# Expert gathers of a decoder step issued from a loop on GpSimd, with rings of 8 and 8 rows

## What is computed

```python
def block_fn(hb):                       # 128 tokens
    q = (hb @ w_q).reshape(PEER_BLOCK, PEER_HEADS, 2, PEER_QDIM // 2).astype(jnp.float32)
    s = jnp.einsum('thpd,phkd->thpk', q, sub_keys.astype(jnp.float32))
    s1, i1 = lax.top_k(s[:, :, 0], PEER_TOPK)
    s2, i2 = lax.top_k(s[:, :, 1], PEER_TOPK)
    ...
    top_s, top_pos = lax.top_k(cand, PEER_TOPK)
    e = jnp.take_along_axis(cidx, top_pos, axis=-1)
    g = jax.nn.softmax(top_s, axis=-1)
    act = jax.nn.gelu(jnp.einsum('thkd,td->thk', u_tab[e], hb).astype(jnp.float32))
    return jnp.einsum('thk,thkd->td', (g * act).astype(hb.dtype), v_tab[e])
```

## Time and profile before

| | us |
|---|---|
| three timed runs: median (lowest to highest) | 1338.03 (1335.47 to 1338.72) |
| the profiled execution, its own time | 1336.01 |
| its span, first to last instruction | 1334.0 |
| first gather starts | 487.89 |
| last gather starts | 1313.11 |

### The profile page before, as it was taken

How to read it: one execution, slowest core, us unless ns; L and a number is a source line. 1 busy time by engine, 2 the same in 40 slices (tenths; PEclk the granted TensorE clock), 3 DMA queues, 4 the chain that set the end, 5 groups by cost and what they waited for, 6 DMA issues and landing times.

```text
span 1334.0 us, 12747 instructions
## 1 busy us (share of the span) xinstructions
PE 1061.0 (80%) x3429; PEld 548.1 (41%) x3429; DVE 711.6 (53%) x1713; ACT 236.3 (18%) x570; POOL 654.9 (49%) x787
## 2 busy tenths in 40 slices
PE   6798888997899895888876877777767777777777
PEld 3346666665577574344322322222222222222223
DVE  3157453887132264688566465457665564443432
ACT  1111221112300210321211211101112112111010
POOL 3333334332000026566666666666666666676663
PEclk9798898998999898888988889899999898999989
DMA  7643341795033569799999999999999999999995
GB/s 241 206 168 105 108 134 48 248 319 164 9 96 126 189 230 384 272 351 357 376 370 369 376 355 369 372 369 398 379 364 366 360 371 370 374 392 356 367 365 215
DMA packets 126412, 379.87 MB, mean 285 GB/s; under 512 B 14284, under 2 KB 23624, under 8 KB 126356
## 3 DMA queue, kind: packets, MB, share of 16 engines
q0 software_dynamic: 89408, 312.89, 61.8%
q1 hardware_dynamic: 36948, 66.29, 14.8%
HBM read 377.55 MB, written 1.59 MB: 284 GB/s over the span
## 4 chain that ended last, share of the span: by engine, by line
PE 46%; POOL 17%; issue 13%; DVE 9%; another core or an unknown queue 6%; DMA 6%; ACT 3%; SPq 0%; DVEq 0%; ACTq 0%; POOLq 0%
PE twoD L838 8%; PE twoD L840 8%; POOL big L966 8%; PE twoA L523 7%; POOL big L955 7%; PE twoA L789 4%; DMA big<-peer_v,oT 3%; PE twoD L740 2%; DVE big L1616 2%; POOL r L955 2%; PE twoA L500 2%; PE twoA L663 1%; PE twoA L460 1%; PE twoD L618 1%
## 5 line engine op out<-in xcount | busy, mean ns | idle before, releaser
L955 POOL DMA_INDIRECT big<-peer_u,oT x232 | 218.8, 943 | 251.3 <-DVEq L1572 165.1
L966 POOL DMA_INDIRECT big<-peer_v,oT x262 | 249.0, 950 | 153.4 <-remote 77.0
L1616 DVE CUSTOM_DVE_ANT_0 big<-big,twoA 128x1024 f32<-128x1024 f32 x128 | 155.2, 1218 | 135.2 <-DMA big<-peer_u,oT 94.1
L1616 DVE CUSTOM_DVE_ANT_0 big<-big,twoD 128x1024 f32<-128x1024 f32 x104 | 124.9, 1214 | 54.5 <-DMA big<-peer_u,oT 28.7
L838 PE MATMUL twoD<-big 128*128 128x512 f32 x176 | 102.1, 659 | 49.7 <-issue 23.1
L523 PE MATMUL twoA<-hT,big 128*128 128x288 f32 x448 | 115.0, 417 | 0.0
L838 PE MATMUL twoD<-big,modT 128*128 128x512 f32 x132 | 79.2, 676 | 39.1 <-DMA big<-peer_v,oT 19.6
L840 PE MATMUL twoD<-big 128*128 128x512 f32 x176 | 96.6, 627 | 8.6 <-issue 8.4
L523 PEld LDWEIGHTS twoA<-hT,big 128*128 128x128 f32 x448 | 86.5, 196 | 24.4 <-issue 0.8
L840 PE MATMUL twoD<-big,modT 128*128 128x512 f32 x132 | 75.9, 654 | 11.6 <-issue 11.4
L838 PEld LDWEIGHTS twoD<-big 128*128 128x128 f32 x176 | 30.7, 199 | 112.8 <-issue 57.9
(11 more groups left out here) (328 smaller groups left out, 1635.9 us busy)
## 6 DMA issues: line engine op xcount, KB each, us to landing
big<-w_ada SPq DMA_DIRECT2D x12, 2048.0 KB, 8.8
big<-w_in SPq DMA_DIRECT2D x5, 2048.0 KB, 8.0
big<-w_in SPq DMA_DIRECT2D x9, 1024.0 KB, 11.3
big<-peer_w_q SPq DMA_DIRECT2D x3, 2048.0 KB, 9.4
big<-peer_v,oT POOLq DMA_INDIRECT x262
big<-cache_v POOLq DMA_DIRECT2D x64, 64.0 KB, 2.1
big<-w_out SPq DMA_DIRECT2D x2, 2048.0 KB, 7.8
big<-peer_u,oT POOLq DMA_INDIRECT x232
```

The source lines that it names most:

```text
L955: pool.indirect_dma_start(urows[i % NU], None, peer_u, bass.IndirectOffsetOnAxis(ap=eidx[:, t, s:s + 1], axis=0)).then_inc(u_in[i % NU], 16)
L966: pool.indirect_dma_start(vrows[j % NV], None, peer_v, bass.IndirectOffsetOnAxis(ap=eidx[:, t, s:s + 1], axis=0)).then_inc(v_in[j % NV], 16)
L1616: dve.tensor_tensor_reduce(out=urows[i % NU], in0=urows[i % NU], in1=h2tok[t][:, :], scale=1.0, scalar=0.0, op0=ALU.mult, op1=ALU.add, acc ...
```

## The change

The rings become 8 and 8 rows, all in `big`. POOL no longer runs an unrolled list: it issues the first 16 u gathers, waits until every weight of the last projection has been used, and then runs an engine loop of 16 passes. A pass has 16 pairs of u(p + 16) and v(p), so v is 16 rounds behind u all through the loop. The last 16 u and the last 32 v follow unrolled, with v catching up. An instruction in a loop can't name another column of `eidx` in each pass, so each stream has a table of 16 columns in `oT`: DVE copies 8 columns at a time into `ucur` (`u_index`), and ACT into `vcur` (`v_index`).

The waits change with it. u(q) waits for `u_used` >= q - 7. v(j) waits for `v_used` >= j + 1, where ACT raises `v_used` by 8 once, behind `exps(0)`; counted in rounds that is j - 7, and no v gather goes ahead of `exps(0)`. `v_index(c+1)`, which stands ahead of `gelus(c+1)` on ACT, waits until round 8c - 1 has been multiplied, which is `v_used` >= 8c counted in rounds. `weigh(c)` now stands behind the dot 8(c+1) + 1.

```diff
-        NU, NV = 10, 11
+        NU, NV = 8, 8
-        LAG, NEAR = 18, 8
+        LAG = 16
...
+            def gather_v(p):
+
+                pool.indirect_dma_start(vrows[p % NV], None, peer_v, bass.IndirectOffsetOnAxis(
+                    ap=vcur[:, p % LAG:p % LAG + 1], axis=0)).then_inc(v_in[p % NV], 16)
...
+            for p in range(LAG):
+                if p % CHUNK == 0:
+                    pool.wait_ge(ucur_ready, p // CHUNK + 1)
+                if p >= NU:
+                    pool.wait_ge(u_used, p - NU + 1)
+                gather_u(p)
+            for g in last_in:
+                pool.wait_ge(*released[g])
+            with pool.Fori(0, ROUNDS // LAG - 2) as i:
+                for p in range(LAG):
...
+                    pool.wait_ge(u_used, i * LAG + (LAG + p - NU + 1))
+                    pool.sem_inc(row_asked, 1)
+                    gather_u(p)
...
+                    pool.wait_ge(v_used, i * LAG + (p + 1))
+                    pool.sem_inc(row_asked, 1)
+                    gather_v(p)
...
             exps(0)
+            act.sem_inc(v_used, NV)
...
+            def v_index(c):
+
+                t, first = slots[c * CHUNK]
+                act.wait_ge(routed, c * CHUNK // (2 * HEAD) + 1)
+                if c >= 2:
+                    act.wait_ge(v_used, NV + (c - 1) * CHUNK)
+                L.tell(act.activation(vcur[:, c % 2 * CHUNK:(c % 2 + 1) * CHUNK], eidx[:, t, first:first + CHUNK], ACT.Copy),
+                       vcur_ready, wait=False)
...
                 if j % CHUNK == CHUNK - 1 and j + 1 < ROUNDS:
+                    v_index(c + 1)
                     gelus(c + 1)
...
+                if i % CHUNK == CHUNK - 1 and i // CHUNK + 2 < ROUNDS // CHUNK:
+                    u_index(i // CHUNK + 2)
+                if i % CHUNK == 1 and i >= CHUNK:
                     weigh(i // CHUNK - 1)
```

More of the change, by code:

```diff
@@ L192, in layer_program @@
         diag = [big[:, NUB * D + 512 + i * P:NUB * D + 512 + (i + 1) * P] for i in range(4)]
-        vrows = [big[:, (NUB + 1 + i) * D:(NUB + 2 + i) * D] for i in range(NV - 1)]
-        v_wring = [0 if (NUB + 2 + i) * D <= o else (1 if (NUB + 2 + i) * D <= o + WSLOT else 2) for i in range(NV - 1)] + [3]
+        vrows = [big[:, (NUB + 1 + i) * D:(NUB + 2 + i) * D] for i in range(NV)]
         diag += [cT[:, 4 * i:4 * i + 4, :].rearrange("p c b -> p (c b)") for i in range(2)]
@@ L271, in layer_program @@
         x1tok = part(3 * D, 0).rearrange("p (t d) -> p t d", d=D)
[L272 to L275, removed]
+        g2tok = part(2 * D, 4 * D).rearrange("p (t d) -> p t d", d=D)
+        yout = part(D, 8 * D)
         adaG = yout.rearrange("p (g n) -> p g n", n=512)
@@ L970, in _, with gather_u @@
[L970 to L978, removed]
+            def gather_u(p):
+                pool.indirect_dma_start(urows[p % NU], None, peer_u, bass.IndirectOffsetOnAxis(
+                    ap=ucur[:, p % LAG:p % LAG + 1], axis=0)).then_inc(u_in[p % NU], 16)
@@ new lines, in _ @@
+            j = ROUNDS - 2 * LAG
+            for i in range(ROUNDS - LAG, ROUNDS):
+                if i % CHUNK == 0:
+                    pool.wait_ge(ucur_ready, i // CHUNK + 1)
+                pool.wait_ge(u_used, i - NU + 1)
+                gather_u(i)
+                while j <= (ROUNDS - CHUNK if i == ROUNDS - 1 else i - LAG + (i - ROUNDS + LAG) // 2):
+                    if j % CHUNK == 0:
+                        pool.wait_ge(vcur_ready, j // CHUNK + 1)
+                    pool.wait_ge(v_used, j + 1)
+                    gather_v(j)
+                    j += 1
@@ L981, in _ @@
+            for j in range(j, ROUNDS):
+                pool.wait_ge(v_used, j + 1)
+                gather_v(j)
         @block.scalar
@@ L1186, in gelus @@
                 L.tell(act.activation(chunk, chunk, ACT.Gelu_apprx_tanh), gelu_done, wait=False)
+            def v_index(c):
[5 more added lines that the diff above has]
+                       vcur_ready, wait=False)
+            v_index(0)
             gelus(0)
@@ L1195, in _ @@
                 if j >= NDG:
-                    act.wait_ge(v_used, j - NDG + 1)
+                    act.wait_ge(v_used, NV + j - NDG + 1)
                 act.activation(diag[j % NDG], ident, ACT.Copy, scale=dots[:, t, s:s + 1]).then_inc(diag_ready, 1)
@@ L1593, in output @@
             def output(t):
-                dve.wait_ge(v_used, sum(SLOTS[0:t + 1]))
+                dve.wait_ge(v_used, NV + sum(SLOTS[0:t + 1]))
                 if t:
@@ L1617, in dot, with u_index @@
                                          op0=ALU.mult, op1=ALU.add, accum_out=dots[:, t, s:s + 1]).then_inc(u_used, 1)
+            def u_index(c):
+                t, first = slots[c * CHUNK]
+                L.tell(cp(ucur[:, c % 2 * CHUNK:(c % 2 + 1) * CHUNK], eidx[:, t, first:first + CHUNK]), ucur_ready, wait=False)
             for _ in route(0):
                 pass
+            u_index(0)
+            u_index(1)
             found, router = 1, route(1)
```

29 lines of the change are left out of this document (10 added, 19 removed).

## The result

| median of 6 runs | us | lowest to highest |
|---|---|---|
| kernel before | 1338.38 | 1335.47 to 1340.48 |
| kernel after | 1351.53 | 1346.97 to 1353.52 |

The ratio is 1.0096, with a 95% interval from 1.0074 to 1.0119. The direction was forecast, the size was not: 64 us were expected and 13 came.

What follows compares the result with a forecast made beforehand. POOL's stalls for late v_used increments while the DMA engines are saturated were taken as the bound. Start +7.4 and stalls 136 + 17 - 95.9 = +57.1 on 1336.01 gave 1400.5, plus 2.0 for the median: 1402.5 us, range 1325 to 1460.

Steps and rivals of the forecast that it cites:

- What bounds the kernel: POOL outpaces the DMA engines; v gathers stall for v_used increments made late by the backlog: 95.9 us in 24 places.
- The rings: v gathers on POOL need v_used three rounds sooner: stalls one in about 8 rounds, 34 x 4.0 = 136 us.
- The restart: The loop's wait is its own instruction, the gather dispatched after it: 0.5 us a stall, 34 x 0.5 = 17 us.
- The tables: Index copies on DVE and ACT cost nothing; v_index's wait mostly falls into the same stall: 0, up to 15 us.
- The start: Fewer gathers go out before the weights are used, but peerq blocks and v(0) come sooner: +7.4 us, -3 to +19.
- The u ring: 8 u rows for 10 leave three rounds of slack and the v wait binds first: nothing, up to 10 us.
- the issue of a gather in a loop: POOL's register instructions cost nothing where its queue is filled: 0, bounds 0 to 0.36 us a gather.
- the tail: Ten v gathers behind the last u, against nine: 0 to 2 us.
- Stalls stay as rare as they were: Rival: POOL's stalls stay at 24 places, of 4.5 us each, plus the start: 1357 us; 15%.
- The transfers are the bound: Rival: 370 GB/s is all the DMA engines have, stalls only move queued work, time stays at 1338 us; 3%.

Runs made afterwards that it cites:

- pace_v_b: Kernel before with a MEMSET of 128x128 ahead of each v gather, on a chip where before takes 1337.73 us: +1.2 us.
- half_pe_c: Kernel before with the first of PE's two matmuls left out in 7 rounds of 8, where before takes 1337.73 us: -8.7 us.
- rings8_late: Kernel before, unrolled, no tables, with 8 u and 8 v rows and v gathers started as late as in after; before 1337.73 us: +1.7 us.
- late_v: Kernel before with only the v start moved: v(0) behind 17 u gathers, all weights used and exps(0); before 1341.86 us: +6.8 us.
- unrolled: Kernel after with the engine loop written out, waits on the gathers against constants; +8.3 us against before at 1257.46, repeated +9.1 against 1257.23.
- unrolled_v3: Kernel after with its loop written out and a v table of 24 columns for 16, v_index waiting for eight rounds less; before 1257.23 us: +9.2 us.
- rings8: Kernel before, unrolled with its old lags, with 8 u and 8 v rows for 10 and 11; before 1257.46 us: +0.3 us.

## Why the prediction was wrong in size

**What bounds the kernel** was right for this chip: stalls of 4 us in which v gathers wait for increments of `v_used` that PE's records show long before. It was half right as to the cause. Busy DMA engines alone don't do it (409 GB/s and 0.04 us on chip A), nor a backlog (17.5 us from issue to landing on chip A, and pace_v_b), nor, as far as chip A and half_pe_c tell, PE's work. It goes with the chip, or with what was different on it at the time. The 93.7 us of stalls, less some 20 that gathers 1.28 us apart and not 1.2425 take on the fast kind, are about the 80 us between the two.

**The rings, +57.1 with the restart: this step failed.** It replayed a cycle of before with the times of the increments held fixed and lowered the threshold by three rounds. The times aren't fixed. In before the increment that a stalled gather needs shows some 22 us late, in after some 15, three rounds less; it is as late as the ring lets it be, and comes when POOL has stopped and all but about one gather has been moved. The term was 34 places x 4.0, 136 us, one in 8 rounds; after measured 28 x 3.75, 105 us, one in 9.7. With rings8_late, which has the rings and neither tables nor loop, it is 24 places as in before, so the rings have none of it that these runs can tell. (The low end of the forecast's own range, 1365 at one in 10 rounds, is 1372 by its terms: 27.2 x 4.5 - 95.9 + 7.4.) The sign that was missed stands in the earlier trace rows: increments 105 to 107 came 4.9 and 9.1 us apart and then all at once. A series that ends in a burst tells when something was let go, not when each step was done, and can't be replayed against another threshold.

**The restart, +17 of these (34 x 0.5)** looks right where the trace shows it. Diagonal 116 and v(112) need the same 105: ACT starts at 851.50 and POOL at 852.29, 0.79 later; `v_index` and v(111) need 104, 845.21 and 845.94, 0.73 later. In before the same pair was 0.23 apart. The traces' semaphore events say the same: from the first increment of the burst to the v gather it is 0.26 us in 27 of before's 28 stalls ahead of v, in 24 of late_v's 26 and 27 of rings8_late's 30, and 0.82 us in 14 of after's 26 and 20 of the 29 on chip B. Some 0.56 us at each of 28 stalls is 16 us at most; the stalls grew by 11.4, and on chip B they are 12.6 us more than late_v's and the time 10. On a chip without stalls it is worth the measured 1.2. But unrolled wasn't run on a chip that stalls. The longer restart is measured; that it, and not the tables, is what the stalls grew by is the likeliest reading and not shown.

**The tables** were put at 0, up to 15. On chip E the place of `v_index`'s wait was worth 0.1 us (unrolled_v3); no run took the copies themselves out. On a chip that stalls `v_index` held ACT for 19.40 us and DVE for 8.56, ending 0.7 us before the start of a v gather that had waited for the same value. In after the stalls stand more often ahead of u (32.1 us for 5.5; 15.8 in rings8_late with the same rings) and less ahead of v. How much of the 11.4 the tables have stays open.

**The start, +7.4 between -3 and +19**: measured about +5.0, with 3.3 of it before the first gather, which the prediction has no term for and which other kernels show without the change. So the number came near in part by luck. v(0) was expected at 531 behind 17 u gathers and came at 527.89 behind 17. The `peerq` blocks come on time, as argued: PE's last record and ACT's last copy are 0.04 us apart, where before had 7.7:

```profile
511.08 11.81 PE L789 MATMUL twoA<-hT,r 128*128 128x288 f32 x48
...
522.93 0.41 ACT L1175 ACTIVATE r<-twoA 128x288 f32<-128x288 f32 x1 [3.47 <-PE twoA L789]
```

On the fast kind, where rings8 (old order at the start) is not late there, the same start costs 8 to 10 us.

**The u ring, the issue of a gather in a loop, the tail**: the first two were put at 0. Gathers stay 1.24 us apart, and rings8_late, with both rings smaller, has no more stalls than late_v, though 15.8 us of them for 9.3 stand ahead of u. The tail, 0 to 2, came out 1.3 shorter. No stall falls on each 16th pair, so no branch is seen.

**The rivals.** "Stalls stay as rare as they were", 1357 with 15%, is nearest to what happened, 5 us from the result. Its argument was the right one: the replay rests on increments that came under the old spacing. Its number is partly luck: 24 x 4.5 = 108 for 28 x 3.75 = 105. "The transfers are the bound", 3%, was put as 370 GB/s being all there is, and the stretch at 412 GB/s dismissed that rightly for this chip; on three of five chips the transfers are the bound, at 409.

**Open**: what delays the increments on some chips, and whether it is the chip at all or something beside this core; whether a pace that leaves the DMA engines idle in between (390 GB/s) would end the stalls there; what sets the 12 to 15 rounds between the long stalls; and how the 11.4 us divide between separate waits and tables.

## What to carry over

A stall whose end is a burst of late signals did not get more frequent here in step with a tighter threshold: before sizing such a term, look whether the signals came one by one as the work was done, or together when something was let go. Where one transfer resource fills a whole stage, first price what a change leaves unmoved at its start; that term was there on both kinds of chip. And run the kernel before on a second chip before explaining its stalls by its program.

## What the chip showed

- One unchanged kernel, 1257 to 1259 us on three chips and 1338 to 1342 on two and on that of the result, the executions on each within 0.6%. The DMA engines moved 409 GB/s over 500 us on the first kind and 370 on the other, where in saturated stretches they also reach 412.
- PE's increments reached ACT 0.04 us after PE's record on the first kind with the DMA engines at 409 GB/s, and 23.4 us after it in the round shown of before, 21.5 in that of pace_v_b, on the second. At the start of after, with the DMA engines at 10 GB/s from 519 to 523 us, they were prompt on the second kind too (0.04 us). How far behind they fall followed the ring there: a median of 22.5 us at the stalls with 11 rows of v, 15.1 with 8.
- POOL has 0.30 us between two gathers. A MEMSET of 128x1 (0.12 us) goes into it for nothing; one of 128x128 (0.23 us) adds about 0.07 (1.32 from a u to the next v and not 1.2425).
- A wait in an instruction of its own let the gather start 0.82 us after the increment in most stalls, where a wait on the gather itself gave 0.26.
